# Latent attention: the query's norm applied as the scale of the softmax exponential, its sums of squares taken with the squares stationary

## The chip, the cores and the metric

One core of one Trainium2 chip runs the whole program as one launch. The metric is device time in microseconds of that core. Five engines work side by side and meet at semaphores: TensorE (PE in the profile, its weight loads PEld), VectorE (DVE), ScalarE (ACT), GpSimd (POOL) and SyncE (SP), which issues the weight transfers.

## The reference

Three transformer blocks over 16 meta tokens and 256 sequence tokens of width 1024, in float32: a state space mixer with an MLP, a latent attention mixer with an MLP, and a block with neighbourhood attention, a convolution branch and an MLP. The change is in the latent attention only:

```python
q = (rms_norm(q_lat, q_a_g) @ w_q_b).reshape(bsz, L, MLA_HEADS, MLA_QK)     # 16 heads of 96
...
q = rms_norm(q, q_norm_g)          # over the 96 values of a head
k = rms_norm(k, k_norm_g)
...                                # rope on the last 32 of the 96
sc = jnp.einsum('bqhd,bkhd->bhqk', q[:, s:e], k[:, :e]).astype(jnp.float32) * scale
p = jax.nn.softmax(jnp.where(mask, sc, -jnp.inf), axis=-1)
```

The norm of the query is one factor per token and head. A row of scores belongs to one query token, so the factor can be applied to the query (before) or to the whole row of scores (after).

## The kernel before

All activations lie transposed, features on the 128 partitions and tokens along the free axis (T = 272 tokens with the meta tokens, T2 = 256 without). A weight page of 128 x 1024 is split into two reduced-precision parts, `w_hi` on ACT and `w_lo` on DVE, and a product is three matmuls (hi x hi, hi x lo, lo x hi). Weight pages pass through four slots.

The latent attention is a hand-written pipeline of 22 steps t (`MLA_STEPS`). Each engine runs its own list of pieces in program order, and semaphores tie the lists together:

- `unit(t)` on PE, t = 0 to 15, makes the raw projection of two heads: keys and values at even t, queries at odd t. `unit_raw` on ACT squares it (`k_sq`, `q_sq`) and copies the value part (`v_t`) or the scaled query part (`q_pre`, L1076). On DVE, `keys` makes the scaled keys `k_pre` (L1560) at even t; `rotate` and `rotate_sum` apply the rope to the query at odd t. PE's next query unit waits for `k_pre` (`kpre_done`), since they share a PSUM bank.
- `unit_norm(t-1)` on PE sums the squares of a head over its 96 rows. For the query (L644) a 97 x 128 matrix of ones is stationary and the squares of 256 tokens move through; row 97 carries the epsilon of the latent's norm. All 128 output rows are the same sum. For the keys (L647) it is done the same way, and three transposes of the values per head (L649 to L651) follow.
- `unit_inv(t-1)` on ACT makes the inverse root: a logarithm (`n_ln`, L1091 for the query, L1096 for the key) and an exponential (`n_inv`, L1108 and L1111), each over 96 rows and 512 or 544 columns. For the keys two copies of the values stand between them. `finish(t-1)` on DVE multiplies: `q_fin` (L1569) and `k_fin` (L1574).
- `scores(t-3)` on PE (L664, L665), `maxima(t-4)` on DVE (L1581: adds the mask to the scores, negates, and keeps the row minimum, `nmx`), `exps(t-4)` on ACT (L1119: two exponentials with the maximum as bias and constant scale -1), `weigh(t-5)` on DVE, `p_transposes(t-6)` on PE (L678 to L682), copies of these to SBUF by ACT (`p_t0_copy`, L1127) and DVE (`p_t_copy`, L1599), `values` on PE for two heads at a time, `o_high` on ACT and `o_low` on DVE.

Order inside a step, which the prediction follows. ACT: `o_high` (even t), `unit_raw`, `p_t0_copy` (odd t, here), `unit_inv`, `exps`, `hi` (the next page's `w_hi`, L839), `p_t0_copy` (even t, here). DVE: `o_low` (even t), `lo` (`w_lo`, L1240), `maxima`, `p_t_copy` (odd t), `keys` or `rotate` with `rotate_sum`, `weigh`, `finish`, `p_t_copy` (even t). PE at even t: `unit`, `unit_norm`, `scores`, `p_transposes`; at odd t: `unit`, `p_transposes`, `unit_norm`, `scores`, `values`.

Of the kernel before, what the change touches and what calls it, by code (L numbers as in the profile page):

```python
# [14 lines left out]
F32 = mybir.dt.float32  # L15
# [131 lines left out]
def build(nc, w, h0, vec, const, rpb, out, acs_dram):  # L147
    ctx = ExitStack()
    with ctx:
# [73 lines left out]
        rot_a = sb("rot_a", [P, 2, T], F32, mla)  # L223
        rot_b = sb("rot_b", [P, 2, T], F32, mla)
        l_ln = rot_a
        q_pre = sb("q_pre", [QK, 4, T2], F32, mla)
        k_pre = sb("k_pre", [QK, 4, T], F32, mla)
        q_sq = sb("q_sq", [QK + 1, 4, T2], F32, mla)
        k_sq = sb("k_sq", [QK, 4, T], F32, mla)
# [103 lines left out]
        lh_done, ll_done, rope_done, krope = sem("lh_done"), sem("ll_done"), sem("rope_done"), sem("krope")  # L333
        raw_read, rot_done, rot_sum, nsum_done = sem("raw_read"), sem("rot_done"), sem("rot_sum"), sem("nsum_done")
        qsq_read, ksq_read, kpre_done = sem("qsq_read"), sem("ksq_read"), sem("kpre_done")
        erow_done, kpesq_done = sem("erow_done"), sem("kpesq_done")
        nln_done, ninv_done, fin_done = sem("nln_done"), sem("ninv_done"), sem("fin_done")
        s_done, sm_done, nm_done, ex_done = sem("s_done"), sem("sm_done"), sem("nm_done"), sem("ex_done")
        ri_done, p_done, pT_done, pt_done, pt0_done = (sem("ri_done"), sem("p_done"), sem("pT_done"),
# [56 lines left out]
        def _(pe):  # L396
# [230 lines left out]
            def unit_norm(un):  # L627

                is_q = un % 2
                ku, k = At(K_HEAD + 2 * un), At(K_HEAD + 2 * un + 1)  # L630
                free(k)
                if is_q:
                    pe.wait_ge(qsq_read, un // 2 + 1)
                    if un == 1:
                        pe.wait_ge(erow_done, 1)
                else:
                    pe.wait_ge(drained[ku.parity], ku.half + 1)
                    if un == 0:
                        pe.wait_ge(kpesq_done, 1)
                for j in range(2):  # L640
                    head = 2 * (un // 2 % 2) + j
                    bank = lin[:, 2 * k.parity + j, :]
                    if is_q:
                        ins = nc.tensor.matmul(bank[:, 0:T2], ones[0:QK + 1, :], q_sq[:, head, :],  # L644
                                               start=True, stop=True)
                    else:
                        nc.tensor.matmul(bank[:, 0:T], ones[0:QK, :], k_sq[:, head, :], start=True, stop=True)  # L647
                        idv = ident[HD:P, HD:P]
                        nc.tensor.transpose(bank[:, 272:336], v_t[HD:P, head, META:144], idv)  # L649
                        nc.tensor.transpose(bank[:, 336:400], v_t[HD:P, head, 144:T], idv)  # L650
                        ins = nc.tensor.transpose(bank[0:META, 400:464], v_t[HD:P, head, 0:META], idv)  # L651
                ins.then_inc(nsum_done, 1)

            def scores(n):
                s, j = n // 4, n % 4
                p = s % 2
                if n % 2 == 0:
                    pe.wait_ge(fin_done, n + 2)
                if n >= 2:
                    pe.wait_ge(sm_done, n - 1)  # L660
                elif n == 0:
                    pe.wait_ge(l_act, 1)
# [168 lines left out]
        def _(act):  # L831
# [237 lines left out]
            def unit_raw(un):  # L1069

                k = At(K_HEAD + 2 * un)
                act.wait_ge(w_used, 2 * C_HEAD + un + 1)
                hs = slice(2 * (un // 2 % 2), 2 * (un // 2 % 2) + 2)
                if un % 2:
                    a(q_sq[0:QK, hs, :], linp(k, slice(0, T2), slice(0, QK)), ACT.Square).then_inc(qsq_read, 1)
                    a(q_pre[0:HD, hs, :], linp(k, slice(0, T2), slice(0, HD)), ACT.Copy,  # L1076
                      scale=v(V_QG, rows=slice(0, HD))).then_inc(drained[k.parity], 1)
                else:
                    a(k_sq[0:HD, hs, :], linp(k, slice(0, T), slice(0, HD)), ACT.Square).then_inc(ksq_read, 1)
                    a(v_t[HD:P, hs, :], linp(k, slice(0, T), slice(HD, P)), ACT.Copy).then_inc(drained[k.parity], 1)  # L1080

            def unit_inv(un):

                s, is_q = un // 4, un % 2
                k = At(K_HEAD + 2 * un + 1)
                w_ = T2 if is_q else T
                if un >= 1:
                    act.wait_ge(ninv_done, un)
                act.wait_ge(nsum_done, un + 1)
                if is_q:  # L1090
                    a(n_ln[:, :, 0:w_], linp(k, slice(0, w_), slice(0, QK)), ACT.Ln, bias=eps_t[0:QK, 3:4],  # L1091
                      scale=1.0 / QK).then_inc(drained[k.parity], 1)
                else:
                    hp = un // 2 % 2
                    hs = slice(2 * hp, 2 * hp + 2)
                    a(n_ln[:, :, 0:w_], linp(k, slice(0, w_), slice(0, QK)), ACT.Ln, bias=eps_t[0:QK, 0:1],  # L1096
                      scale=1.0 / QK)
                    if s >= 2:
                        act.wait_ge(pv_done, 4 * (s - 2) + 2 * hp + 2)
                    a(v_tok[s % 2][:, hs, 1:3, :], linp(k, slice(272, 400)).rearrange("p h (t d) -> p h t d", d=HD),  # L1100
                      ACT.Copy)
                    a(v_tok[s % 2][0:META, hs, 0, :], linp(k, slice(400, 464), slice(0, META)), ACT.Copy)\
                        .then_inc(drained[k.parity], 1)
                act.wait_ge(drained[k.parity], k.half + 1)
                if un >= 1:
                    act.wait_ge(fin_done, un)
                if is_q:
                    a(n_inv[:, :, 0:w_], n_ln[:, :, 0:w_], ACT.Exp, scale=-0.5, bias=eps_t[0:QK, 1:2])\  # L1108
                        .then_inc(ninv_done, 1)
                else:  # L1110
                    a(n_inv[:, :, 0:w_], n_ln[:, :, 0:w_], ACT.Exp, scale=-0.5).then_inc(ninv_done, 1)  # L1111

            def exps(n):
                p = n % 2
                act.wait_ge(sm_done, n + 1)
                if n >= 3:
# [117 lines left out]
        def _(dve):  # L1234
# [310 lines left out]
            def rotate_sum(t):  # L1545

                un, h0_ = t // 2, 2 * (t // 2 % 2)
                dve.wait_ge(rot_done, 2 * un + 1)
                nc.vector.tensor_copy(rot_b[rr, :, 0:T2], rot_a[rs_, :, 0:T2]).then_inc(rot_done, 1)
                dve.wait_ge(rot_done, 2 * un + 2)  # L1550
                tt(q_pre[rr, h0_:h0_ + 2, :], rot_a[rr, :, 0:T2], rot_b[rr, :, 0:T2], ALU.add).then_inc(rot_sum, 1)

            def keys(t):

                un, h0_ = t // 2, 2 * (t // 2 % 2)
                k = At(K_HEAD + 2 * t)
                dve.wait_ge(ksq_read, un + 1)
                if t >= 4:
                    dve.wait_ge(fin_done, t - 3)
                ts(k_pre[0:HD, h0_:h0_ + 2, :], linp(k, slice(0, T), slice(0, HD)),  # L1560
                   v(V_KG, rows=slice(0, HD)), None, ALU.mult).then_inc(kpre_done, 1)

            def finish(un):
                s = un // 4
                dve.wait_ge(ninv_done, un + 1)
                hs = slice(2 * (un // 2 % 2), 2 * (un // 2 % 2) + 2)
                if un % 2:
                    dve.wait_ge(rot_sum, un // 2 + 1)
                    ins = tt(q_fin[s % 2][:, hs, :], q_pre[:, hs, :], n_inv[:, :, 0:T2], ALU.mult)  # L1569
                else:  # L1570
                    dve.wait_ge(kpre_done, un // 2 + 1)
                    if un == 0:
                        dve.wait_ge(krope, 3)
                    ins = tt(k_fin[s % 2][:, hs, :], k_pre[:, hs, :], n_inv[:, :, :], ALU.mult)  # L1574
                ins.then_inc(fin_done, 1)

            def maxima(n):
                p, o = n % 2, (ps5, ps6)[n % 2]
                dve.wait_ge(s_done, n + 1)
                for i, sl in enumerate((slice(0, 144), slice(144, 416))):  # L1580
                    ins = nc.vector.tensor_tensor_reduce(  # L1581
                        out=s_m[p][:, sl], in0=o[:, sl], in1=cst[:, N_MLA + sl.start:N_MLA + sl.stop], scale=-1.0,
                        scalar=3e38, op0=ALU.add, op1=ALU.min, accum_out=nmx[p][:, i:i + 1])
                ins.then_inc(sm_done, 1)

            def weigh(n):
                p = n % 2
# [17 lines left out]
            for t in range(MLA_STEPS + 1):  # L1605
# [394 lines left out]
```

## Time and profile before

| | us |
|---|---|
| median of 3 runs (lowest, highest) | 1151.34 (1149.97, 1151.72) |
| the profiled execution's own time | 1150.44 |
| its span, first to last instruction | 1148.8 |
| PE busy in the span | 1111.8 (97%) |
| PEld, DVE, ACT, POOL busy | 1068.5, 766.3, 672.6, 152.2 |
| mean granted clock of TensorE | 0.996 of 2.4 GHz |

The span is 1.6 us shorter than the profiled execution's time, and that execution is 0.9 us below the median. The latent attention's pipeline of steps lies at 477 to 590 us of the span. There PE was busy for 99.81 of 113.00 us, ACT for 81.63 and DVE for 78.99. Times in the rows are microseconds from the start of the span.

### The profile page before, as it was taken

The page shows a single profiled execution, that of the slowest core. Times are in us where ns is not written, and L with a number is a line of the kernel's source. Part 1 is how long each engine was busy: PE and PEld are TensorE (multiplying, and loading weights), DVE is VectorE, ACT ScalarE, POOL GpSimd, SP SyncE. Part 2 cuts the span into 40 slices and gives each one's busy share as a digit, 9 for nine tenths or more (in the row PEclk, how much of TensorE's full clock was granted, in tenths as well). Part 3 has the DMA queues.
Part 4 walks back from the last instruction along what each step waited for, and adds up shares of the span by engine and source line. Part 5 has one row for each costly group of instructions (what it writes and reads, how often), then busy time and mean ns, then how long its engine had stood idle before and what let it go on. Part 6 is the DMA issues. An engine that isn't in the chain of part 4 may idle for free.

```text
span 1148.8 us, 23776 instructions
## 1 busy us (share of the span) xinstructions
PE 1111.8 (97%) x8898; PEld 1068.5 (93%) x8898; DVE 766.3 (67%) x1122; ACT 672.6 (59%) x1071; POOL 152.2 (13%) x118
## 2 busy tenths in 40 slices
PE   6999999999999999899889999999999999999998
PEld 5989999999999999877689999999998999999998
DVE  4689999767665555678766665555687577666443
ACT  4789999655454434688655554445545656555332
POOL 0344443417000000100010000000001302000000
PEclk9999999999999999999999999999999999999999
DMA  5554454484555555333235555565544556555552
GB/s 201 172 181 164 150 185 147 139 247 165 183 170 177 165 182 175 123 110 108 74 108 186 183 185 188 175 197 172 174 138 128 189 175 188 188 184 186 191 183 91
DMA packets 53225, 190.32 MB, mean 166 GB/s; under 512 B 5920, under 2 KB 7072, under 8 KB 53168
## 3 DMA queue, kind: packets, MB, share of 16 engines
q1 hardware_dynamic: 51408, 182.95, 48.9%
q0 software_dynamic: 1760, 6.59, 1.8%
q8 instruction: 38, 0.62, 0.2%
q14 instruction: 19, 0.16, 0.0%
HBM read 188.44 MB, written 1.08 MB: 165 GB/s over the span
## 4 chain that ended last, share of the span: by engine, by line
PE 89%; DVE 6%; ACT 3%; issue 1%; DMA 0%; SPq 0%; ACTq 0%; DVEq 0%
PE lin L414 27%; PE lin L416 27%; PE lin L415 27%; DVE w_lo L1240 2%; ACT w_hi L839 1%; PE ps L507 1%; PE lin L647 1%; PE ps L447 1%; DVE x_lo L1250 0%; PE ps L665 0%; DVE cv L1320 0%; ACT pr L1167 0%; PE ps L695 0%; PE ps L693 0%; PE ps L510 0%
## 5 line engine op out<-in xcount | busy, mean ns | idle before, releaser
L1240 DVE TENSOR_TENSOR w_lo<-w_raw,w_hi 128x1024 fp32r<-128x1024 f32 (+2 forms) x319 | 387.2, 1215 | 281.4 <-ACT w_hi L839 281.2
L839 ACT ACTIVATE w_hi<-w_raw 128x1024 fp32r<-128x1024 f32 (+1 forms) x343 | 355.0, 1039 | 236.1 <-PE lin L416 234.1
L414 PE MATMUL lin<-x_hi,w_hi 128*128 128x256 f32 (+1 forms) x1528 | 442.7, 290 | 10.8 <-DVE cv L1320 4.1
L416 PE MATMUL lin<-x_hi,w_lo 128*128 128x256 f32 (+1 forms) x1528 | 436.6, 286 | 0.0
L415 PE MATMUL lin<-x_lo,w_hi 128*128 128x256 f32 (+1 forms) x1528 | 435.8, 285 | 0.0
L414 PEld LDWEIGHTS lin<-x_hi,w_hi 128*128 128x128 f32 x1528 | 289.5, 189 | 14.9 <-DVE cv L1320 4.6
L415 PEld LDWEIGHTS lin<-x_lo,w_hi 128*128 128x128 f32 x1528 | 289.0, 189 | 1.4 <-issue 1.0
L416 PEld LDWEIGHTS lin<-x_hi,w_lo 128*128 128x128 f32 x1528 | 289.8, 190 | 0.0
L416 PE MATMUL lin<-hid_hi,w_lo 128*128 128x256 f32 (+1 forms) x768 | 218.2, 284 | 0.0
L415 PE MATMUL lin<-hid_lo,w_hi 128*128 128x256 f32 (+1 forms) x768 | 217.9, 284 | 0.0
L414 PE MATMUL lin<-hid_hi,w_hi 128*128 128x256 f32 (+1 forms) x768 | 217.4, 283 | 0.0
L416 PEld LDWEIGHTS lin<-hid_hi,w_lo 128*128 128x128 f32 x768 | 145.2, 189 | 0.0
L414 PEld LDWEIGHTS lin<-hid_hi,w_hi 128*128 128x128 f32 x768 | 145.0, 189 | 0.0
L415 PEld LDWEIGHTS lin<-hid_lo,w_hi 128*128 128x128 f32 x768 | 144.4, 188 | 0.0
L1773 POOL TENSOR_TENSOR h_sq<-h_sq 128x256 f32<-128x256 f32 (+1 forms) x35 | 31.1, 890 | 554.1 <-ACT h_sq L852 552.7
L1007 ACT ACTIVATE relu<-lin 128x512 f32<-128x512 f32 (+1 forms) x48 | 29.1, 605 | 82.7 <-PE lin L416 82.7
L1784 POOL TENSOR_TENSOR w_lo<-w_raw,w_hi 128x1024 fp32r<-128x1024 f32 x24 | 59.0, 2459 | 86.1 <-ACT w_hi L839 86.0
L848 ACT ACTIVATE x_hi<-h,vecs 128x256 fp32r<-128x256 f32 (+2 forms) x40 | 20.3, 508 | 42.7 <-DVE h L1480 37.7
L1463 DVE TENSOR_TENSOR hid_lo<-relu_sq,hid_hi 128x512 f32 (+1 forms) x48 | 34.4, 717 | 11.2 <-DVE relu_sq L1459 11.2
L1320 DVE SCALAR_TENSOR_TENSOR cv<-lin,vecs,cv 128x271 f32<-128x271 f32 (+2 forms) x96 | 40.1, 477 | 0.0
L414 PE MATMUL lin<-g_hi,w_hi 128*128 128x272 f32 x128 | 37.8, 295 | 1.9 <-DVE g_lo L1364 1.0
L416 PE MATMUL lin<-g_hi,w_lo 128*128 128x272 f32 x128 | 37.0, 289 | 0.0
(265 smaller groups left out, 1469.5 us busy)
## 6 DMA issues: line engine op xcount, KB each, us to landing
w_raw<-w SPq DMA_DIRECT2D x343, 512.0 KB, 3.4
acs_bc<-acs_dram POOLq DMA_DIRECT2D x8, 544.0 KB, 4.9
bias_mask<-rpb POOLq DMA_DIRECT2D x4, 512.0 KB, 9.7
h<-h SPq DMA_DIRECT2D x4, 272.0 KB, 4.1
out<-h SPq DMA_DIRECT2D x8, 128.0 KB, 3.2
cst<-const SPq DMA_DIRECT2D x1, 784.0 KB, 8.9
vecs<-vec SPq DMA_DIRECT2D x1, 131.5 KB, 2.2
acs_dram<-y POOLq DMA_DIRECT2D x1, 34.0 KB, 2.1
```

The source lines that it names most:

```text
L414: mm3(o, wh, xh, start=first and i == 0, stop=False)
L415: mm3(o, wh, xl, start=False, stop=False)
L416: ins = mm3(o, wl, xh, start=False, stop=last and i == kts - 1)
L447: ins = nc.tensor.matmul(ps7[:, 0:T], ones0, h_sq[:, kt, :], start=kt == 0, stop=kt == KD - 1)
L839: a(w_hi[pg.slot][:, 0:n], w_raw[pg.slot][:, 0:n], ACT.Copy).then_inc(w_hi_done, pages)
L848: a(x_hi[:, kt.value, 0:width(norm)], h[:, kt.value, tokens(norm)], ACT.Copy, scale=gain(norm, kt.value)).then_inc(xh_done, 1)
L1007: a(relu[i][:, :, 0:n], linp(k, slice(0, n)), ACT.Relu).then_inc(drained[k.parity], 1)
L1240: tt(w_lo[pg.slot][:, 0:n], w_raw[pg.slot][:, 0:n], w_hi[pg.slot][:, 0:n].bitcast(F32), ALU.subtract)\
L1320: ins = stt(cv[:, q, back:T], lin[:, 2 * k.parity + i, 0:T - back], v(s.times(20, V_CONV + 5 * q + 3 - back).value), cv[:, q, back:T], ALU ...
L1463: tt(hid_lo[:, bass.ds(at.value, 2), 0:n], relu_sq[i][:, :, 0:n], hid_hi[:, bass.ds(at.value, 2), 0:n].bitcast(F32), ALU.subtract).then_in ...
L1773: tt(h_sq[:, 0, 0:n], h_sq[:, 0, 0:n], h_sq[:, kt, 0:n], ALU.add).then_inc(hsum_done, 1)
L1784: tt(w_lo[pg.slot][:, 0:n], w_raw[pg.slot][:, 0:n], w_hi[pg.slot][:, 0:n].bitcast(F32), ALU.subtract)\
```

## The change

The query is no longer normalized before the scores. `unit_raw` and `rotate_sum` write the scaled and rotated query straight into `q_fin`, and the multiplication L1569 is gone. The sums of squares are taken with the squares of 128 tokens stationary and one column of ones moving, so that they come out with tokens on the partitions: four matmuls of one column for two heads in place of two of 256 columns. The logarithm and exponential of `unit_inv` work on 128 x 4 values in place of 96 x 512. The scores are raw; `maxima` keeps the row maximum in `mx`, and a small added instruction multiplies it by minus the norm's factor `q_inv`, giving the bias; `exps` takes `q_inv` as its scale, a column of 128 values in place of the constant. The semaphores follow: `fin_done` counts keys only, and `scores` waits for the raw query's two parts.

```diff
+        q_ln = sb("q_ln", [P, 2, 2], F32, mla)
+        q_inv = sb("q_inv", [P, 8, 2], F32, mla)
+        mx = [sb(f"mx{i}", [P, 2], F32, mla) for i in range(2)]
...
                     if is_q:
-                        ins = nc.tensor.matmul(bank[:, 0:T2], ones[0:QK + 1, :], q_sq[:, head, :],
-                                               start=True, stop=True)
+                        for qt in range(2):
+                            at = 2 * j + qt
+                            ins = nc.tensor.matmul(lin[:, 2 * k.parity, at:at + 1],
+                                                   q_sq[:, head, qt * P:(qt + 1) * P], ones[0:QK + 1, 0:1],
+                                                   start=True, stop=True)
...
                 if n % 2 == 0:
-                    pe.wait_ge(fin_done, n + 2)
+                    kq = At(K_HEAD + 2 * (n + 1))
+                    pe.wait_ge(fin_done, n // 2 + 1)
+                    pe.wait_ge(rot_sum, n // 2 + 1)
+                    pe.wait_ge(drained[kq.parity], kq.half + 1)
...
-                    a(q_pre[0:HD, hs, :], linp(k, slice(0, T2), slice(0, HD)), ACT.Copy,
+                    if s >= 2:
+                        act.wait_ge(s_done, 4 * (s - 2) + hs.stop)
+                    a(q_fin[s % 2][0:HD, hs, :], linp(k, slice(0, T2), slice(0, HD)), ACT.Copy,
                       scale=v(V_QG, rows=slice(0, HD))).then_inc(drained[k.parity], 1)
...
                 if is_q:
-                    a(n_ln[:, :, 0:w_], linp(k, slice(0, w_), slice(0, QK)), ACT.Ln, bias=eps_t[0:QK, 3:4],
-                      scale=1.0 / QK).then_inc(drained[k.parity], 1)
+                    if un >= 2:
+                        act.wait_ge(qinv_done, un // 2)
+                    a(q_ln[:, :, :].rearrange("p h t -> p (h t)"), lin[:, 2 * k.parity, 0:4], ACT.Ln,
+                      bias=eps_t[:, 3:4], scale=1.0 / QK).then_inc(drained[k.parity], 1)
...
                 if is_q:
-                    a(n_inv[:, :, 0:w_], n_ln[:, :, 0:w_], ACT.Exp, scale=-0.5, bias=eps_t[0:QK, 1:2])\
-                        .then_inc(ninv_done, 1)
+                    at = 2 * (un // 2 % 4)
+                    a(q_inv[:, at:at + 2, :], q_ln[:, :, :], ACT.Exp, scale=-0.5, bias=eps_t[:, 1:2])\
+                        .then_inc(qinv_done, 1)
...
-                    ins = a(pr[n % 3][:, sl], s_m[p][:, sl], ACT.Exp, scale=-1.0, bias=nmx[p][:, i:i + 1],
+                    ins = a(pr[n % 3][:, sl], s_m[p][:, sl], ACT.Exp, scale=q_inv[:, n % 8, i:i + 1],
+                            bias=nmx[p][:, i:i + 1],
                             accum_out=rsum[p][:, i:i + 1])
...
-                tt(q_pre[rr, h0_:h0_ + 2, :], rot_a[rr, :, 0:T2], rot_b[rr, :, 0:T2], ALU.add).then_inc(rot_sum, 1)
+                s = t // 4
+                if s >= 2:
+                    dve.wait_ge(s_done, 4 * (s - 2) + h0_ + 2)
+                tt(q_fin[s % 2][rr, h0_:h0_ + 2, :], rot_a[rr, :, 0:T2], rot_b[rr, :, 0:T2], ALU.add)\
+                    .then_inc(rot_sum, 1)
...
-                if un % 2:
-                    dve.wait_ge(rot_sum, un // 2 + 1)
-                    ins = tt(q_fin[s % 2][:, hs, :], q_pre[:, hs, :], n_inv[:, :, 0:T2], ALU.mult)
...
-                        out=s_m[p][:, sl], in0=o[:, sl], in1=cst[:, N_MLA + sl.start:N_MLA + sl.stop], scale=-1.0,
-                        scalar=3e38, op0=ALU.add, op1=ALU.min, accum_out=nmx[p][:, i:i + 1])
-                ins.then_inc(sm_done, 1)
+                        out=s_m[p][:, sl], in0=o[:, sl], in1=cst[:, N_MLA + sl.start:N_MLA + sl.stop], scale=1.0,
+                        scalar=-3e38, op0=ALU.add, op1=ALU.max, accum_out=mx[p][:, i:i + 1])
+                ins.then_inc(mx_done, 1)
+                dve.wait_ge(qinv_done, n // 2 + 1)
+                dve.wait_ge(mx_done, n + 1)
+                stt(nmx[p][:, :], mx[p][:, :], -1.0, q_inv[:, n % 8, :], ALU.mult, ALU.mult).then_inc(sm_done, 1)
...
-                if 1 <= t <= 16:
+                if 1 <= t <= 16 and t % 2:
                     finish(t - 1)
```

## Rows read from the trace of the kernel before

**Rows 1.** Waits of 476 to 592 us: total us, times, longest us.

```profile
PE ps L678 <- ACT p_t L1127: 4.4, 4, 3.3
PE lin L414 <- DVE k_pre L1560: 1.8, 1, 1.8
```

**Rows 2.** Stretches: length, busy us (instructions) of PE, PEld, DVE, ACT, POOL; PEclk, DMA.

```profile
530.90:542.16 11.26, 10.87 (x74) 8.23 (x75) 9.37 (x26) 9.33 (x24) 0.00 (x0) 1.00 0.28 95
560.00:570.00 10.00, 6.15 (x35) 4.97 (x33) 6.77 (x20) 5.23 (x15) 0.00 (x0) 0.83 0.33 106
```

**Rows 3.** PE in order of time: start us, us, line and operation, count.

```profile
508.06 0.28 PE L416 MATMUL lin<-l_hi,w_lo 128*128 128x256 f32 x1
508.40 0.27 PE L678 MATMUL ps<-cst,pr 128*16 128x128 f32 x1
...
530.15 0.28 PE L415 MATMUL lin<-l_lo,w_hi 128*128 128x256 f32 x1
530.26 0.28 PE L416 MATMUL lin<-l_hi,w_lo 128*128 128x256 f32 x1
530.91 0.27 PE L678 MATMUL ps<-cst,h_sq 128*16 128x128 f32 x1 [0.37 <-ACT p_t L1127]
...
537.20 1.03 PE L644 MATMUL lin<-q_sq,cst 97*128 97x256 f32 x4
538.06 0.41 PE L664 MATMUL ps<-k_fin,q_fin 96*128 96x144 f32 x2
538.31 0.62 PE L665 MATMUL ps<-k_fin,q_fin 96*128 96x272 f32 x2
...
539.21 0.27 PE L682 MATMUL ps<-cst,pr 128*128 128x128 f32 x1
539.41 0.36 PE L414 MATMUL lin<-l_hi,w_hi 128*128 128x256 f32 x1
```

**Rows 4.** ACT in order of time, one pair of steps.

```profile
533.47 0.71 ACT L1096 ACTIVATE n_ln<-lin,eps_t 96x544 f32<-96x544 f32 x1 [1.40 <-PE lin L651]
534.35 0.25 ACT L1102 ACTIVATE v_tok<-lin 16x128 f32<-16x128 f32 x1
538.68 0.68 ACT L1091 ACTIVATE n_ln<-lin,eps_t 96x512 f32<-96x512 f32 x1
540.02 0.40 ACT L1119 ACTIVATE h_sq<-s_m,nmx 128x144 f32<-128x144 f32 x1
541.66 0.35 ACT L1127 ACTIVATE p_t<-ps 16x256 f32<-16x256 f32 x1
```

**Rows 5.** DVE in order of time: the maximum's last piece and what follows it.

```profile
538.54 0.09 DVE L1581 DVE_READ_ACCUMULATOR2_ANT nmx<- 128x1 f32 x1
538.54 0.77 DVE L1560 TENSOR_SCALAR k_pre<-lin,vecs 64x544 f32<-64x544 f32 x1
```

**Rows 6.** DVE in the later neighbourhood attention, where a maximum is negated.

```profile
831.50 0.08 DVE L1645 DVE_READ_ACCUMULATOR2_ANT mx<- 128x1 f32 x1
831.62 0.17 DVE L1650 TENSOR_SCALAR nmx<-mx 128x2 f32<-128x2 f32 x1
831.70 1.00 DVE L1713 SCALAR_TENSOR_TENSOR cv<-zc,vecs,cv 128x256 f32<-128x256 f32 x2
```

**Rows 7.** ACT by form, whole span: count | busy us, mean ns | idle before.

```profile
L909 ACT ACTIVATE cv<-lin,vecs 128x272 f32<-128x272 f32 x32 | 16.4, 563 | 0.0
L963 ACT ACTIVATE g_ln<-ps,eps_t 128x272 f32<-128x272 f32 x8 | 3.9, 482 | 5.2 <-PE ps L494 5.2
```

**Rows 8.** DVE and PE at the last gated query unit.

```profile
550.74 0.77 DVE L1560 TENSOR_SCALAR k_pre<-lin,vecs 64x544 f32<-64x544 f32 x1
551.62 0.36 PE L414 MATMUL lin<-l_hi,w_hi 128*128 128x256 f32 x1 [0.89 <-issue]
```

**Rows 9.** The tail: ACT, then PE, in order of time.

```profile
562.54 0.41 ACT L1119 ACTIVATE pr<-s_m,nmx 128x144 f32<-128x144 f32 x1 [0.88 <-DVE nmx L1581]
564.91 0.27 PE L678 MATMUL ps<-cst,h_sq 128*16 128x128 f32 x1 [3.27 <-ACT p_t L1127]
```

More of the change, by code:

```diff
@@ L225, in build @@
         l_ln = rot_a
-        q_pre = sb("q_pre", [QK, 4, T2], F32, mla)
+        q_ln = sb("q_ln", [P, 2, 2], F32, mla)
+        q_inv = sb("q_inv", [P, 8, 2], F32, mla)
+        mx = [sb(f"mx{i}", [P, 2], F32, mla) for i in range(2)]
         k_pre = sb("k_pre", [QK, 4, T], F32, mla)
@@ L335, in build @@
         qsq_read, ksq_read, kpre_done = sem("qsq_read"), sem("ksq_read"), sem("kpre_done")
-        erow_done, kpesq_done = sem("erow_done"), sem("kpesq_done")
+        erow_done, kpesq_done, qinv_done, mx_done = sem("erow_done"), sem("kpesq_done"), sem("qinv_done"), sem("mx_done")
         nln_done, ninv_done, fin_done = sem("nln_done"), sem("ninv_done"), sem("fin_done")
@@ L1074, in unit_raw @@
                 if un % 2:
+                    s = un // 4
                     a(q_sq[0:QK, hs, :], linp(k, slice(0, T2), slice(0, QK)), ACT.Square).then_inc(qsq_read, 1)
-                    a(q_pre[0:HD, hs, :], linp(k, slice(0, T2), slice(0, HD)), ACT.Copy,
+                    if s >= 2:
+                        act.wait_ge(s_done, 4 * (s - 2) + hs.stop)
+                    a(q_fin[s % 2][0:HD, hs, :], linp(k, slice(0, T2), slice(0, HD)), ACT.Copy,
                       scale=v(V_QG, rows=slice(0, HD))).then_inc(drained[k.parity], 1)
@@ L1085, in unit_inv @@
                 k = At(K_HEAD + 2 * un + 1)
-                w_ = T2 if is_q else T
-                if un >= 1:
-                    act.wait_ge(ninv_done, un)
                 act.wait_ge(nsum_done, un + 1)
                 if is_q:
-                    a(n_ln[:, :, 0:w_], linp(k, slice(0, w_), slice(0, QK)), ACT.Ln, bias=eps_t[0:QK, 3:4],
-                      scale=1.0 / QK).then_inc(drained[k.parity], 1)
-                else:
+                    if un >= 2:
+                        act.wait_ge(qinv_done, un // 2)
+                    a(q_ln[:, :, :].rearrange("p h t -> p (h t)"), lin[:, 2 * k.parity, 0:4], ACT.Ln,
+                      bias=eps_t[:, 3:4], scale=1.0 / QK).then_inc(drained[k.parity], 1)
+                else:
+                    if un >= 2:
+                        act.wait_ge(ninv_done, un // 2)
                     hp = un // 2 % 2
                     hs = slice(2 * hp, 2 * hp + 2)
-                    a(n_ln[:, :, 0:w_], linp(k, slice(0, w_), slice(0, QK)), ACT.Ln, bias=eps_t[0:QK, 0:1],
+                    a(n_ln[:, :, :], linp(k, slice(0, T), slice(0, QK)), ACT.Ln, bias=eps_t[0:QK, 0:1],
                       scale=1.0 / QK)
@@ L1104, in unit_inv @@
                 act.wait_ge(drained[k.parity], k.half + 1)
-                if un >= 1:
-                    act.wait_ge(fin_done, un)
                 if is_q:
-                    a(n_inv[:, :, 0:w_], n_ln[:, :, 0:w_], ACT.Exp, scale=-0.5, bias=eps_t[0:QK, 1:2])\
-                        .then_inc(ninv_done, 1)
-                else:
-                    a(n_inv[:, :, 0:w_], n_ln[:, :, 0:w_], ACT.Exp, scale=-0.5).then_inc(ninv_done, 1)
+                    at = 2 * (un // 2 % 4)
+                    a(q_inv[:, at:at + 2, :], q_ln[:, :, :], ACT.Exp, scale=-0.5, bias=eps_t[:, 1:2])\
+                        .then_inc(qinv_done, 1)
+                else:
+                    if un >= 2:
+                        act.wait_ge(fin_done, un // 2)
+                    a(n_inv[:, :, :], n_ln[:, :, :], ACT.Exp, scale=-0.5).then_inc(ninv_done, 1)
             def exps(n):
@@ L1558, in keys @@
                 if t >= 4:
-                    dve.wait_ge(fin_done, t - 3)
+                    dve.wait_ge(fin_done, t // 2 - 1)
                 ts(k_pre[0:HD, h0_:h0_ + 2, :], linp(k, slice(0, T), slice(0, HD)),
@@ L1564, in finish @@
                 s = un // 4
-                dve.wait_ge(ninv_done, un + 1)
+                dve.wait_ge(ninv_done, un // 2 + 1)
                 hs = slice(2 * (un // 2 % 2), 2 * (un // 2 % 2) + 2)
-                if un % 2:
-                    dve.wait_ge(rot_sum, un // 2 + 1)
-                    ins = tt(q_fin[s % 2][:, hs, :], q_pre[:, hs, :], n_inv[:, :, 0:T2], ALU.mult)
[L1570 to L1575, printed above, removed]
+                dve.wait_ge(kpre_done, un // 2 + 1)
+                if un == 0:
+                    dve.wait_ge(krope, 3)
+                tt(k_fin[s % 2][:, hs, :], k_pre[:, hs, :], n_inv[:, :, :], ALU.mult).then_inc(fin_done, 1)
             def maxima(n):
```

## The prediction

> **What bounds the kernel now.** I read the page's busy shares first: PE is busy for 97% of the span, so over the whole program only what moves PE counts. The change touches only the latent attention's steps, 113 us long. There I read the waits, and then laid one pair of steps (a key unit and a query unit) out engine by engine.
>
> One pair takes 11.26 us, and PE is busy for 10.87 of them, ACT for 9.33 and DVE for 9.37 [rows 2]. PE waits once per pair in plain sight, for ACT's small copy of the transposed probabilities before L678 [rows 1, 3]. The last matmul of the query unit starts at 530.26 and L678 at 530.91, which is 0.65 us; a matmul of this kind hands over after 0.11 to 0.12 us [rows 3], so 0.53 us are lost. The same gap stands ahead of 519.66 and 542.16, and a smaller one of 0.34 - 0.12 = 0.22 us ahead of 508.40 [rows 3].
>
> The second gate is nearly hidden. Each query unit waits for DVE's `k_pre`. In the pair shown `k_pre` starts at 538.54 and lasts 0.77 us, so it ends at 539.31, and the unit starts at 539.41 [rows 3, 5]. At the last query unit it ends at 551.51, and the unit starts at 551.62, 0.11 us later [rows 8]; there the profile calls the 0.89 us of idle time "issue", but the constant lag to `k_pre` tells what it is. The six query units 5, 7, ... 15 all start 0.10 or 0.11 us after the end of `k_pre`. In three of them (9, 11, 13) PE would itself have been ready only some 0.1 us earlier (L682 starts at 539.21 and holds PE for 0.11), in the others it idles longer. So whatever makes `k_pre` later moves PE one for one, and whatever makes it earlier gives almost nothing in those three.
>
> What stands before `k_pre`? PE's last value transpose L651 releases ACT, which had been idle for 1.40 us [rows 4]. ACT then makes the key's `n_ln`, two copies, `n_inv`, the two exponentials of `exps`, `w_hi` and `o_hi`; DVE follows with `o_lo`, `w_lo`, the maximum, and `k_pre`. None of the query's norm lies in this chain. It lies in the other one, from the end of PE's key unit through ACT's `k_sq`, `v_t`, query `n_ln`, `n_inv`, `exps`, `w_hi` and the copy L1127 to PE's L678.
>
> **The change part by part.** *The query's norm on ACT.* From the start of `n_ln` at 538.68 to the start of `exps` at 540.02 are 1.34 us [rows 4]. Two instructions of 4 columns take their place. The trace has none of that size with 128 partitions; the nearest is the copy of 16x128 at 0.25 us [rows 4]. I take 0.25 each, 0.5 for both with the wait between them, so 0.84 goes. The ends are nothing for both and 0.7 (0.08 more each for the bias column, worked out below), so between 0.64 and 1.34 goes. Of this `exps` gives 0.16 back (below). PE's gap of 0.53 needs no more than 0.53, and PE itself comes later by the terms that follow, so the gap closes at either end. What is late next at L678 is PE itself. The relief is 3 x 0.53 + 0.22 = **-1.8 us**. After the last query unit, in the tail, ACT's query norm lies in time in which ACT then waits for the maximum anyway (0.88 us idle [rows 9]), and gives nothing.
>
> *The multiplication L1569 on DVE* (0.69 us, eight times) stands behind `k_pre` and `weigh`; the copy behind it lies 0.3 us ahead of PE. It hides behind PE and gives nothing to the gates. Writing into `q_fin` straight away costs the same as into `q_pre`. Its new waits, for scores of two head groups earlier, and those of `scores` for the raw query of two steps earlier, were met long before: nothing.
>
> *The small instruction after the maximum.* In the later attention the same pattern exists: the read-out starts at 831.50, the negation at 831.62, the next instruction at 831.70 [rows 6]. Before, `k_pre` starts with the read-out (both 538.54 [rows 5]), so the price is 0.20 us in front of `k_pre`. Its ends are 0.08 (if the wait cost nothing) and 0.35 (the 0.12 of the wait, the whole 0.17 of the instruction and another wait of 0.05, since two semaphores are waited for). I take 0.20, the same pattern. Queued behind it on DVE are `k_pre`, for which PE waits, and everything up to `weigh`. It is paid at query units 5, 7, 9, 11, 13, 15, and once in the tail, where ACT waits for the maximum [rows 9] and PE for ACT (3.27 us [rows 9]): 7 x 0.20 = **+1.4 us**.
>
> *The scale of the exponential as a column.* An activation of 128x272 from PSUM with scale and bias columns takes 563 ns, one with the bias column alone 482 [rows 7]: 0.08 us per instruction, with an end of 0 (another function and output might explain the difference) and of 0.1. Two exponentials stand in the chain before `k_pre` of query units 7, 9, 11, 13, 15, and four in the tail's chain (one pair delays `w_hi`, `o_hi` and `w_lo`, the next, at 562.54 [rows 9], stands before L1127): 14 x 0.08 = **+1.1 us**. The Trainium skill states this price (ScalarE: Activation LUTs, section What ACT_TABLE_LOAD costs): each column operand adds about 93 ns over an immediate. It speaks against the change, and the trace's 81 ns bears it out; by the page's figure this term would be 1.3 us and my sum 0.2 us higher.
>
> *The sums on PE.* Before, four matmuls (each product of plain float32 takes two) from 537.20 to 538.06, 0.86 us [rows 3]. After, eight, each with its own load of 97x128. The nearest pitch with such a load is that of L664, 0.25 us for two at 144 columns [rows 3], so 8 x 0.125 = 1.0 us by this row. No row has one moving column: the low end is nothing at all, the high end 0.27 each (the whole duration of L678 [rows 3]), 2.2 us. I take 1.0, +0.14 for each query unit, as the same load decides it. It doesn't show: between the sums and the next query unit PE is going to wait for `k_pre`, 0.1 us already and 0.36 more by the two terms above, so 0.45 of cover. Cheaper matmuls would be hidden by the same wait. Were the cover gone, it would be 8 x 0.14 = 1.1 us.
>
> **Sum.** -1.8 + 1.4 + 1.1 = +0.7 us against the profiled execution's 1150.44, 1151.1 us. Since that execution lies 0.9 below the median of 1151.34, the forecast for the median is 1152.0. ACT would be less busy by about 5 us and DVE by about 3, and PE would not gain.
>
> **The rivals.** *A: the late chain has slack that I don't see*, and the relief stays whole, with the small instruction and the scale column hidden: 1151.34 - 1.8 = 1149.5. For it: ACT and DVE are busy for only 83% of a pair [rows 2]. Against it: the constant 0.1 us lag at six units.
>
> *B: the one-column matmuls are dear.* On PE, between the query's squares and the next `scores`: if load and multiplication of one column don't overlap as those of 144 columns do, each takes a pitch p of its own. The cover of 0.45 is used up from 8p = 0.86 + 0.45, p = 0.163 us. At the high end, p = 0.27, each of some seven units adds 2.16 - 1.31 = 0.85, and the time is 1152.0 + 5.9 = 1157.9. Against it: L664 has 0.125 with the same load. The Trainium skill (TensorE: Matmul & The Clock Gate, section LDWEIGHTS) prices a load of 128 columns at 107 ns whatever the rows, which would make eight of them 0.86 us, no change; no row here has one moving column.
>
> *C: the relief doesn't come*, because L678 waits for DVE's copy and the probabilities once ACT is out of the way, while all prices are paid: 1151.34 + 2.5 = 1153.8. It decides if that copy ends over 0.3 us later than now in relation to PE's query unit. Against it: 0.69 us of multiplication goes from in front of it.
>
> *D: the clock.* After PE's idle 3.3 us in the tail the granted clock is 0.83 on average at 560 to 570 [rows 2], as 3.4 us at the lower level (1.2 GHz) give it, and PE loses 10 x 0.17 = 1.7 us of work. If that stretch isn't there after the change: 1152.0 - 1.7 = 1150.3. If PE's longer waits bring a second one, 1153.7.
>
> **How the numbers follow.** Forecast 0.55, its own range 1151.2 to 1152.9 (the ends of the wait and of the scale column). A 0.18, B 0.08, C 0.08, D without the stretch 0.07, with a second 0.04. A measurement of this kernel tells 0.2%, 2.3 us, from no change, so faster is below 1149.0 and slower above 1153.6. Slower: half of B's, C's and the second stretch's 0.20, and a little of the forecast's upper end, 0.13. Faster: the lower end of A and A with D, 0.06. Same 0.81. The range 1149.4 to 1153.9 takes in A, most of C and D, and leaves out B.
>
> **What would show it.** Right: the wait of L678 for ACT's L1127 shrinks from 4.4 us to the tail's alone, 3.3 to 3.7; query units start 0.10 us after `k_pre`, and that starts 0.2 us after the read-out; L1119 at 272 columns goes from 507 to about 590 ns; a pair of steps takes 11.1 us. Wrong: a pair of 10.7 us (A), a pitch over 0.16 us in L644's successors (B), L678 waiting for DVE (C). The prediction is wrong as a whole if the attention's steps change by more than 2 us either way.

## The result and the profile after

The changed kernel takes 1155.12 us (median of 6 executions, 1153.89 to 1156.76) against 1151.17 us for the kernel before, timed beside it: a ratio of 1.0033 with a 95% interval of [1.0023, 1.0043]. It is slower by 3.9 us, where 0.7 was forecast, and lies above the range's end of 1153.9. A second comparison (e1 below) gives 1.0026 [1.0015, 1.0038], 3.0 us.

The profiled execution took 1154.64 us (span 1153.0), 4.2 us above the one of before; 0.7 of them had come about before the attention's first query unit (478.56 against 477.81), the rest lies in the attention. ACT's 669.3 busy us are 3.3 fewer and DVE's 764.3 are 2.0 fewer, somewhat less than the 5 and 3 forecast. PE's 1116.3 are 4.5 more, which no part of the sum had. First the waits of 476 to 592 us:

```profile
PE ps L686 <- ACT p_t L1141: 3.7, 1, 3.7
PE lin L416 <- issue: 4.7, 6, 1.4
PE lin L416 <- DVE k_pre L1578: 1.8, 1, 1.8
```

Of four waits for ACT's small copy [rows 1] only the tail's is left. The six waits put down to "issue" are the query units, which now visibly wait for the key scaling. One pair of steps on PE (start us, us, what, idle before):

```profile
533.29 0.28 PE L418 MATMUL lin<-l_hi,w_lo 128*128 128x256 f32 x1
533.41 0.27 PE L686 MATMUL ps<-cst,h_sq 128*16 128x128 f32 x1
...
539.70 0.95 PE L648 MATMUL lin<-cst,q_sq 97*128 97x1 f32 x8
540.51 0.49 PE L672 MATMUL ps<-k_fin,q_fin 96*128 96x144 f32 x2
...
541.73 0.27 PE L690 MATMUL ps<-cst,pr 128*128 128x128 f32 x1
542.34 0.36 PE L416 MATMUL lin<-l_hi,w_hi 128*128 128x256 f32 x1 [0.33 <-issue]
```

L686 follows the query unit's last matmul after 0.12 us, where it took 0.65 [rows 3]: the relief is whole. Eight one-column products take 0.81 us (539.70 to 540.51), 0.10 each, a little less than the 0.86 of before. The query unit starts 0.61 us after L690, where it took 0.20 [rows 3]. DVE at the same place:

```profile
541.17 0.08 DVE L1594 DVE_READ_ACCUMULATOR2_ANT mx<- 128x1 f32 x1
541.35 0.16 DVE L1600 SCALAR_TENSOR_TENSOR nmx<-mx,q_inv 128x2 f32<-128x2 f32 x1
541.46 0.78 DVE L1578 TENSOR_SCALAR k_pre<-lin,vecs 64x544 f32<-64x544 f32 x1
```

The key scaling starts 0.29 us after the last read-out, not with it [rows 5], and ends at 542.24, 0.10 before PE's unit. The two prices on ACT (by form, 476 to 592 us: count | busy, mean ns | idle before):

```profile
L1132 ACT ACTIVATE pr<-s_m,nmx,q_inv 128x272 f32<-128x272 f32 x11 | 6.6, 599 | 0.0
L1119 ACT ACTIVATE q_inv<-q_ln,eps_t 128x4 f32<-128x4 f32 x8 | 2.4, 297 | 0.3
L1101 ACT ACTIVATE q_ln<-lin,eps_t 128x4 f32<-128x4 f32 x8 | 2.1, 262 | 0.2
```

The exponential of 272 columns went from 507 ns to 599, and the query's pair of activations to 0.26 and 0.30 us.

So far everything is as argued, but for the small instruction's 0.29 us in place of 0.20. What the sum didn't have stands in the clock (stretches of 5 and 12 us: length, busy us of PE, PEld, DVE, ACT, POOL with instructions, PEclk, DMA share, GB/s). Before:

```profile
497.00:502.00 5.00, 5.00 (x35) 3.98 (x35) 3.89 (x10) 3.93 (x10) 0.00 (x0) 1.00 0.45 156
562.00:574.00 12.00, 9.09 (x60) 7.79 (x60) 6.78 (x26) 5.01 (x16) 0.00 (x0) 0.86 0.28 88
```

and after:

```profile
497.00:502.00 5.00, 4.75 (x24) 4.25 (x25) 2.20 (x8) 2.36 (x6) 0.00 (x0) 0.66 0.54 192
562.00:574.00 12.00, 7.60 (x41) 6.22 (x40) 6.61 (x21) 5.68 (x16) 0.00 (x0) 0.72 0.26 88
```

At 497 to 502 the granted clock is 0.66 on average, 3.4 us at 1.2 GHz where before had none, and in the tail it is 0.72 in place of 0.86, 6.8 us at the lower level in place of 3.4. PE makes 24 matmuls in the first stretch in place of 35.

To compare kernels free of what happens in the program's start I use the **stage**: from the start of query unit 1 (477.81 before) to the first matmul after PE's last wait of the attention (590.33 before). Before it is 112.5 us, after 594.55 - 478.56 = 116.0. In the table each median has the kernel before's, timed beside it, in brackets; the ratio is taken over the executions and isn't the quotient of the two medians (in e6 it is 0.9998, the quotient 0.9993).

| kernel | median us (before beside it) | ratio [95%] | stage us | low-clock stretches in the stage: start (length) |
|---|---|---|---|---|
| before | 1151.17 | | 112.5 | 565 (3.4) |
| after | 1155.12 (1151.17) | 1.0033 [1.0023, 1.0043] | 116.0 | 498 (3.4), 566 (6.8) |
| e1 after again | 1154.59 (1151.6) | 1.0026 [1.0015, 1.0038] | 115.9 | 496 (3.4), 564 (6.8) |
| e2 128 moving columns | 1153.71 (1151.6) | 1.0020 [1.0011, 1.0028] | 113.8 | 567 (3.4) |
| e3 prices only | 1154.00 (1151.6) | 1.0022 [1.0013, 1.0031] | 115.7 | 567 (6.8) |
| e4 before, one column | 1154.32 (1151.6) | 1.0024 [1.0012, 1.0035] | 115.2 | 497 (3.4), 565 (6.8) |
| e5 e2, keys first | 1152.51 (1151.07) | 1.0010 [1.0002, 1.0019] | 113.6 | 567 (3.4) |
| e6 before, keys first | 1150.25 (1151.07) | 0.9998 [0.9989, 1.0006] | 112.0 | 565 (3.4) |
| e7 e6, step 16 | 1150.80 (1151.07) | 1.0001 [0.9992, 1.0010] | 111.6 | 565 (3.4) |
| e8 e5, step 16 | 1151.08 (1151.07) | 1.0000 [0.9991, 1.0009] | 114.9 | 479 (3.4), 564 (6.8) |
| e9 wide at unit 3 alone | 1154.57 (1151.42) | 1.0032 [1.0020, 1.0045] | 116.9 | 488 (3.4), 509 (3.4), 567 (6.8) |
| e10 one column at unit 3 alone | 1154.55 (1151.42) | 1.0035 [1.0021, 1.0048] | 116.0 | 498 (3.4), 566 (6.8) |
| e11 32 columns | 1154.69 (1151.42) | 1.0030 [1.0018, 1.0042] | 115.9 | 498 (3.4), 566 (6.8) |
| e12 e2, negated on GpSimd | 1152.17 (1151.42) | 1.0005 [0.9996, 1.0014] | 113.3 | 563 (6.8) |

The stretches come from one profiled execution each. A second look at them is the mean granted clock over all timed executions: 0.9937 to 0.9942 for the kernel before (76 executions beside e1 to e12; three far slower ones, 1215 to 1345 us at a mean clock of 0.76 to 0.85, are left out), 0.990 to 0.991 for each of the kernels with narrow sums (after, e1, e4, e9, e10, e11), 0.992 to 0.994 for e2, e3, e5 to e8 and e12. The executions also split the difference without any trace: at a mean clock of 0.993 the four of the changed kernel (after and e1) average 1153.7 us and the 31 of the kernel before 1152.0. So about 1.7 us of the 3.0 to 3.9 are there at equal clock, and the rest goes with the clock. This is an estimate, since the clock is on record to 0.001 and that much goes with 0.5 us (the kernel before averages 1150.5 at 0.996).

### The profile page after: what moved, and what is told of

Same layout as the page of the kernel before. It is cut to its first block, busy times and chain, and to the rows that moved or that the text cites. A ratio compares the mean times of both kernels' runs of the same rounds, so it can differ in the third digit from the quotient of the medians.

```text
span 1153.0 us, 23859 instructions
## 1 busy us (share of the span) xinstructions
PE 1116.3 (97%) x8930; PEld 1074.6 (93%) x8930; DVE 764.3 (66%) x1130; ACT 669.3 (58%) x1071; POOL 152.3 (13%) x118
## 4 chain that ended last, share of the span: by engine, by line
PE 91%; DVE 5%; ACT 2%; issue 1%; DMA 0%; SPq 0%; ACTq 0%; DVEq 0%
PE lin L416 28%; PE lin L418 27%; PE lin L417 27%; DVE w_lo L1254 2%; PE ps L509 1%; ACT w_hi L847 1%; PE lin L652 1%; PE ps L449 1%; PE ps L673 0%; DVE cv L1334 0%; ACT pr L1181 0%; PE ps L672 0%; PE ps L703 0%; PE ps L701 0%; PE lin L648 0%
## 5 line engine op out<-in xcount | busy, mean ns | idle before, releaser
L1254 DVE TENSOR_TENSOR w_lo<-w_raw,w_hi 128x1024 fp32r<-128x1024 f32 (+2 forms) x319 | 387.1, 1215 | 283.1 <-ACT w_hi L847 282.8
L1477 DVE TENSOR_TENSOR hid_lo<-relu_sq,hid_hi 128x512 f32 (+1 forms) x48 | 34.4, 716 | 11.2 <-DVE relu_sq L1473 11.2
```

Source lines behind the costliest of these rows:

```text
L1254: tt(w_lo[pg.slot][:, 0:n], w_raw[pg.slot][:, 0:n], w_hi[pg.slot][:, 0:n].bitcast(F32), ALU.subtract)\
L1477: tt(hid_lo[:, bass.ds(at.value, 2), 0:n], relu_sq[i][:, :, 0:n], hid_hi[:, bass.ds(at.value, 2), 0:n].bitcast(F32), ALU.subtract).then_in ...
```

## The experiments

My theory once the two traces lay side by side: the gates behave as predicted, and the rest is the clock, which falls where PE's sums have one moving column and stand next to a wait. The rivals: the added prices lengthen PE's waits and that lowers the clock, or the difference lies in the start of the program, where the two traces differ too.

**e1.** No edit.

> The changed kernel once more, for a second trace and for the clock of more executions. Its first trace has 6.8 us at the lower clock in the attention's tail and 3.4 us at 498 to 501 us, where the kernel before had 3.4 and none. Theory 'clock' (the change makes PE fall to 1.2 GHz more often in the attention's steps): the ratio is again 1.003 to 1.004, and a low stretch lies somewhere among the head units again. Rival 'start' (the low stretches of the program's first 60 us, which differ between the two traces, make the difference, by luck of one build or one chip): the ratio falls to 1.001, and the mean clock of the executions is that of the kernel before (0.995).

The ratio fell a little, but stays clear of 1.001, and the stretch is there again at 496. In this trace the start has 3.4 us twice, as in the kernel before, and the stage is the same as in the first (115.9). So the start is not the cause of what the stage shows.

**e2.** 128 columns move through.

```diff
-                            at = 2 * j + qt
+                            at = (2 * j + qt) * P
-                            ins = nc.tensor.matmul(lin[:, 2 * k.parity, at:at + 1],
-                                                   q_sq[:, head, qt * P:(qt + 1) * P], ones[0:QK + 1, 0:1],
+                            ins = nc.tensor.matmul(lin[:, 2 * k.parity, at:at + P],
+                                                   q_sq[:, head, qt * P:(qt + 1) * P], ones[0:QK + 1, :],
...
-                    a(q_ln[...], lin[:, 2 * k.parity, 0:4], ACT.Ln, ...
+                    a(q_ln[...], lin[:, 2 * k.parity, 0:4 * P:P], ACT.Ln, ...
```

> The changed kernel with 128 identical moving columns of ones in place of one in the query's sums (ACT reads every 128th column of the result). PE then works for the full 0.86 us per query unit, not 0.8 us with one column per load. Theory 'one column' (products of one column count as idle for the clock): the extra low stretches vanish and the time is 1.0 to 1.5 us above the kernel before (1152 to 1152.7). Rival 'waits' (the added price before the key scaling and in the tail lengthens PE's waits, and that brings the low clock): as the changed kernel, 1155.

The stretch is gone:

```profile
497.00:502.00 5.00, 3.99 (x27) 2.95 (x25) 3.44 (x11) 3.56 (x9) 0.00 (x0) 1.00 0.46 126
562.00:574.00 12.00, 7.60 (x47) 5.84 (x46) 6.61 (x21) 5.35 (x16) 0.00 (x0) 0.86 0.28 88
```

Query unit 7 starts 10.1 us after unit 5; in after it is 11.65, so the stretch costs 1.5 us. The whole stage is 113.8, 1.2 us above before: that is the change without its added low-clock stretches. By medians the kernel is still 2.1 us above before, not 1.5 at most, and only 0.9 below e1, with intervals that overlap: the times alone don't show what the wide sums give back, the stage does. Its trace has 3.4 us of low clock at 595, just behind the stage, which the kernel before doesn't have, and its executions have a lower mean clock (0.992).

**e3.** The two prices on the kernel before.

```diff
-                        ..., scale=-1.0, scalar=3e38, op0=ALU.add, op1=ALU.min, accum_out=nmx[p][:, i:i + 1])
-                ins.then_inc(sm_done, 1)
+                        ..., scale=1.0, scalar=-3e38, op0=ALU.add, op1=ALU.max, accum_out=mx[p][:, i:i + 1])
+                ins.then_inc(mx_done, 1)
+                dve.wait_ge(ninv_done, 2 * (n // 2) + 2)
+                dve.wait_ge(mx_done, n + 1)
+                stt(nmx[p][:, :], mx[p][:, :], -1.0, cst[:, N_ONES:N_ONES + 2], ALU.mult, ALU.mult)...
...
-                    ins = a(..., ACT.Exp, scale=-1.0, bias=nmx[p][:, i:i + 1], ...
+                    ins = a(..., ACT.Exp, scale=cst[:, N_ONES:N_ONES + 1], bias=nmx[p][:, i:i + 1], ...
```

> The kernel before with the two prices alone: the maximum kept positive and negated by a small instruction, and the exponential's scale as a column (of ones). The norm stays on the query as before. By the sum of the prediction, with the measured 0.29 us for the small instruction in place of 0.20: 7 x 0.29 + 14 x 0.09 = +3.3 us, less nothing, since the gap at the small copy stays: 1154.5. Theory 'waits' for the clock: 1.7 to 3.4 us more, 1156 to 1158, with a low stretch among the head units. Theory 'one column': 1154.5 without one.

1154.0 for 1154.5, and no stretch at 497, although PE idles longer ahead of query units 5 and 7 (1.09 and 1.51 us) than in the changed kernel (1.01 and 1.44):

```profile
497.00:502.00 5.00, 4.39 (x30) 3.49 (x31) 3.49 (x9) 3.85 (x9) 0.00 (x0) 1.00 0.39 111
```

A pair of steps takes 11.45 us, 0.2 more than before, not 0.47: as the query unit comes later, PE's wait for ACT shrinks by itself. Its matmul after the query unit:

```profile
532.65 0.28 PE L417 MATMUL lin<-l_hi,w_lo 128*128 128x256 f32 x1
533.02 0.27 PE L679 MATMUL ps<-cst,h_sq 128*16 128x128 f32 x1
```

0.37 us here, 0.65 before [rows 3], 0.12 after. This tells what the shorter norm on ACT is worth once the prices are paid: 0.25 of the 0.53 us; the rest went by the lateness alone. In the tail this trace has 6.8 us at the low clock in place of 3.4, without narrow sums.

**e4.** The one-column matmuls of the change in the kernel before (the hunk of `unit_norm` alone). The kernel leaves the query's norm out in effect, since the logarithm still reads the place where the wide sums stood.

> The kernel before with the query's sums made as in the changed kernel (squares stationary, one moving column, four numbers per pair of heads); the logarithm then reads mostly old values of the bank, so this kernel leaves the query's norm out in effect, and all durations and waits but PE's stay. Theory 'one column': slower by 1.7 to 3.5 us, 1153 to 1154.7, with a low stretch among the head units or a longer one in the tail. Rival 'waits': no change, 1151.2, since PE's sums are hidden behind its wait for the scaled keys.

```profile
493.87 0.95 PE L646 MATMUL lin<-cst,q_sq 97*128 97x1 f32 x8
494.68 0.49 PE L667 MATMUL ps<-k_fin,q_fin 96*128 96x144 f32 x2
495.01 0.62 PE L668 MATMUL ps<-k_fin,q_fin 96*128 96x272 f32 x2
496.39 0.36 PE L414 MATMUL lin<-l_hi,w_hi 128*128 128x256 f32 x1 [0.76 <-issue]
```

```profile
497.00:502.00 5.00, 5.00 (x26) 3.89 (x25) 3.29 (x9) 2.59 (x7) 0.00 (x0) 0.66 0.43 160
```

The one edit makes the kernel 2.7 us slower and brings the stretch, with PE's idle time ahead of the query unit as before (0.76 us, 0.78 before). The sums themselves take 0.81 us, less than before. Nothing but the sums was edited, so the 2.7 us (1.4 to 4.0 by the interval) are theirs. Of the stage's 2.6 us, 1.5 go with the stretch at 497 (query unit 7 starts 11.24 us after unit 5, 9.70 before) and 1.0 with the longer one in the tail.

**e5.** DVE, even steps: `keys(t)` moved ahead of `maxima(t - 4)`, on e2.

> The changed kernel with 128 moving columns (as e2) and, on DVE at even steps, the key scaling ahead of the maximum. Theory 'gate' (the price of the small instruction and of the scale column is paid at the key scaling, for which each later query unit waits): 0.9 us leave that chain, so query units 5, 7 and 15 start 0.9 us earlier and 9, 11, 13 by the 0.4 us that PE idles there; the maximum comes later and ACT's small copy with it, which takes back 0.2 us three times. In all -3.2 us against e2, 1150.5. Rival 'elsewhere' (the prices are paid at L678 or on ACT): -1 us or less, 1152.7 or more.

The chain to the key scaling did shorten: query unit 5 starts 8.3 us after unit 3 (9.1 in e2), unit 7 another 9.4 (10.1). But the stage is only 0.2 us shorter. PE's wait for ACT came back; from matmul to matmul it is 0.70 us, where I had reckoned with some 0.3:

```profile
542.37 0.28 PE L418 MATMUL lin<-l_hi,w_lo 128*128 128x256 f32 x1
543.07 0.27 PE L686 MATMUL ps<-cst,pr 128*16 128x128 f32 x1 [0.43 <-ACT p_t L1141]
```

and the way from query unit 15 to the tail's L686 takes 15.0 us, 1.1 more. Both ends of the expectation missed: the gate is real, but right behind it ACT holds the pair at 11.2 us.

**e6.** The same move in the kernel before.

> The kernel before with the key scaling ahead of the maximum at even steps. Theory 'gate': query units 5, 7 and 15 start 0.6 us earlier, 9, 11 and 13 are held by L678's wait for ACT anyway: -1.8 us, 1149.8. If instead the lag of 0.10 us to the key scaling is a coincidence: no change. The difference between e5 and this kernel is what the change is worth once the gate is away: by the theory -1.6 to 0 us for the norm on the scale (the relief at L678), plus 0.09 us per exponential in the tail.

The stage is 0.6 us shorter and the ratio holds no difference. Units 5 and 7 come earlier, by 0.6 us each as expected, so the lag was no coincidence, but the pairs stay at 11.26 us, and unit 9 (0.4 us) and the tail's L678 (0.7) give part of it back. Of the 1.8 us expected, 0.6 came.

**e7, e8.** In step 16 the maximum ahead of `lo`, the small copy ahead of `hi`, on e6 and e5.

> e6 and, in step 16 alone, the maximum ahead of the weight part on DVE and the small copy ahead of the weight part on ACT. PE's idle stretch before the tail's L678 shrinks from 3.3 to about 1.3 us. If idle time of PE is what brings the low clock in the tail, the 3.4 us at 1.2 GHz after it vanish: -2.0 - 1.7 = -3.7 us against e6, 1146.1. If the low stretch stays, -2.0, 1147.8.

> e5 with the same reordering of step 16. The tail's idle stretch goes from 3.9 to about 1.5 us: -2.4 for the wait and -1.7 to -2.4 for the low clock, 1146.1 against e5's 1150.5. With the gate away and the clock kept, the change should be level with e7 or up to 1 us faster; if it is slower than e7 by over 1 us, something beside the gates and the clock is paid.

Neither came: e7 takes 1150.8 us where at most 1147.8 was expected, e8 1151.1 for 1146.1. In e8, for one, the matmul that waited 3.72 us for ACT in the changed kernel now waits for DVE's copy:

```profile
565.18 0.37 PE L686 MATMUL ps<-cst,h_sq 128*16 128x128 f32 x1 [2.38 <-DVE p_t L1617]
```

The wait in e7 fell by 0.6 us only, the low stretch stayed at 3.4 us in e7 and at 6.8 in e8, and the medians are level with the kernel before. e8's trace also has a low stretch at 479, ahead of the first query sums: it begins 1.5 us behind a wait of 1.8 us that all kernels have. So narrow sums are not the only way to a low stretch. The tail's clock was not cured, and these two tell nothing sure on it.

**e9, e10.** The width chosen by unit: `wide = P if un == 3 else 1`, and `1 if un == 3 else P`.

> The changed kernel with 128 moving columns in the sums of query unit 3 alone, the last sums before PE waits for the start of query unit 5, and one column in the other seven. Theory 'one column next to a wait' (one-column products and the wait after them together let PE look idle): no low stretch at 496 to 501 us; time as e2, 2.1 to 2.4 us above the kernel before. Rival 'one column anywhere': the stretch stays, 3.0 us above.

> The reverse: one moving column in the sums of query unit 3 alone, 128 in the other seven. Theory 'one column next to a wait': the low stretch of 3.4 us at 496 to 501 is there, query unit 7 starts 11.6 us after query unit 5 instead of 10.1, and the time is that of the changed kernel, 3.0 us above the kernel before. Rival 'one column anywhere' (the sum of all eight units' missing work counts): no stretch, 2.2 above.

e9, five stretches from 487 us:

```profile
487.00:492.00 5.00, 3.49 (x17) 3.52 (x18) 2.33 (x3) 2.18 (x5) 0.00 (x0) 0.66 0.45 130
...
497.00:502.00 5.00, 3.98 (x29) 3.23 (x29) 3.48 (x13) 3.66 (x10) 0.00 (x0) 1.00 0.35 108
...
507.00:512.00 5.00, 3.57 (x20) 3.24 (x18) 4.66 (x16) 3.57 (x10) 0.00 (x0) 0.69 0.35 105
```

e10:

```profile
487.00:492.00 5.00, 4.01 (x28) 3.15 (x28) 2.75 (x5) 2.86 (x6) 0.00 (x0) 1.00 0.56 174
...
497.00:502.00 5.00, 4.86 (x24) 4.38 (x25) 2.17 (x8) 2.33 (x5) 0.00 (x0) 0.66 0.54 190
...
507.00:512.00 5.00, 3.57 (x29) 3.07 (x27) 4.59 (x17) 3.93 (x11) 0.00 (x0) 1.00 0.32 105
```

The stretch follows the narrow sums. With unit 3 wide it left 497 and came up behind the waits after units 1 and 5, whose sums are narrow in e9. With unit 3 alone narrow it is at 498 and nowhere else among the units. e9's time of 1.0032 was not foreseen (I expected e2's), since I hadn't thought of the other two waits.

Yet narrow sums next to a wait don't bring the stretch each time. PE idles for 0.7 us or more ahead of query units 3, 5, 7 and 15. Over all traces there are 20 such places behind sums with 1 or 32 columns, and 7 have a low stretch that begins within 0.7 us of the query unit's start; in the changed kernel only the one at unit 5 has it, though the waits at 3, 7 and 15 are longer. There are 24 such places behind sums with 128 or 256 columns, and none has it. What decides between the places with narrow sums stays open.

**e11.** `wide = 32`.

> The changed kernel with 32 moving columns in all query sums. PE's pitch stays that of the load, 0.10 us a product, as with one column (64 passes in 6.5 us against 6.9 us at 128 columns). If it is the columns that pass which keep the clock, a quarter of the work may be too little and the stretch at 496 to 501 stays (11.6 us from query unit 5 to 7); if any real stream of columns does, it goes (10.1 us).

```profile
497.00:502.00 5.00, 4.32 (x21) 3.99 (x21) 2.29 (x7) 2.26 (x6) 0.00 (x0) 0.66 0.56 166
```

In this trace 32 columns do no more for the clock than one.

**e12.** The negation and multiplication on GpSimd, as two small instructions in place of one, on e2. GpSimd had nothing to do in these steps. `maxima` gets two waits more, so that it doesn't overwrite what is still read.

```diff
-                dve.wait_ge(qinv_done, n // 2 + 1)
-                dve.wait_ge(mx_done, n + 1)
-                stt(nmx[p][:, :], mx[p][:, :], -1.0, q_inv[:, n % 8, :], ALU.mult, ALU.mult).then_inc(sm_done, 1)
...
+                for i in range(2):
+                    ins = ts(nmx[p][:, i:i + 1], mx[p][:, i:i + 1], q_inv[:, n % 8, i:i + 1], -1.0,
+                             ALU.mult, ALU.mult)
+                ins.then_inc(sm_done, 1)
```

> [...] The 0.29 us of the small instruction leave the chain to the key scaling: DVE's key scaling starts with the read-out again, and query units 5 and 7 each start 0.29 us sooner after the one before (8.84 and 9.84 us in place of 9.13 and 10.13). But the bias reaches ACT later by what GpSimd needs beyond DVE. If that is under 0.3 us the exponentials at even steps hardly wait, and the time is 1 to 1.7 us below e2; if it is 0.5 us or more, PE's wait moves to L678's successor and the gain is under 0.5 us.

DVE's key scaling starts with the read-out again:

```profile
538.99 0.08 DVE L1597 DVE_READ_ACCUMULATOR2_ANT mx<- 128x1 f32 x1
538.99 0.77 DVE L1578 TENSOR_SCALAR k_pre<-lin,vecs 64x544 f32<-64x544 f32 x1
```

Units 5 and 7 start 8.85 and 9.83 us after the ones before, as expected to 0.01 us, and the median is 0.8 us above before in place of e2's 2.1. The tail gives some back: the way from unit 15 to its L686 is 14.7 us, 13.85 in e2. The pairs take 10.87 us, 0.4 less than before: with the small instruction off DVE the relief does show. In the tail its trace has 6.8 us at the low clock. This form is level with the kernel before [0.9996, 1.0014], as is e8 [0.9991, 1.0009]; no form of the change beat it.

## Why the prediction was wrong

*The relief* was sized 0.53 us a pair and came whole; the wait is gone in all four places. e3 shows that half of it would have come by lateness alone, a point that the sum didn't need.

*The small instruction* was put at 0.20 us and costs 0.29, within its ends. The neighbourhood attention's pattern has one wait, here there are two; that this is the reason was not tested. 7 x 0.09 = 0.6 us of the miss.

*The scale column* was put at 0.08 per instruction and costs 0.09 (599 - 507 ns).

*The sums on PE* are the step that failed. Their duration lay inside its bounds (0.81 us against the 1.0 I took, and 0.86 before) and it was hidden, as I wrote. From "it doesn't show" I concluded that the step costs nothing. It costs the clock: e4 has the sums alone and loses 2.7 us by medians, 2.6 in the stage.

*The gates together* were to give +0.7. Without the clock's part they gave 1.2 (the stage of e2), close to +0.7 with the 0.6 of the small instruction. By medians e2 is 2.1 us above before; the 0.9 us that its stage doesn't hold stay open.

*Rival D*, the clock, named a second low stretch and its price of 1.7 us, but put it down to longer waits and gave it 0.04. e3 has longer waits and no stretch at 497; e4 has the same waits and the stretch. Of the others, A wanted a pair of 10.7 us and it is 11.15, B a pitch over 0.16 us and it is 0.10, C a wait of L686 for DVE and there is none in the pairs. My sign for being wrong as a whole, steps that change by more than 2 us, did come: 3.5.

Of the stage's 3.5 us, then, 1.2 are gates, 1.5 the stretch at 497, and 0.7 the longer one in the tail (10.60 us from its L686 at 568.28 to the next that waits, 578.88; 9.91 in e2, 9.97 before). This sum, from one trace, agrees with the medians' 3.0 and 3.9. That narrow sums at unit 3 bring the stretch at 497 is settled: it is there in all five traces with narrow sums at unit 3 (after, e1, e4, e10, e11) and in none of the nine others. Five of these nine (before, e2, e3, e9, e12) have PE idle there for 0.7 to 1.1 us as well; e5 to e8 hardly have the wait. Why the tail's stretch is 6.8 us in some kernels and 3.4 in others stays open. All six traces with narrow sums have 6.8, e10 too, whose sums near the tail are wide; e4 has 6.8 with the idle time of before, e3 and e12 have 6.8 with wide sums, e2 and e5 have 3.4 with idle time as long as e3's; one execution each can't tell it.

## What to carry to other kernels

A matmul's time in the profile is not all that it does: products with few moving columns look busy (0.95 us here) but next to a wait they can let PE's clock fall, and the price is paid by the matmuls that follow. When an edit makes PE's work lighter in a stage where PE also waits, price the clock as a term of its own, and look at PEclk in 5 us stretches before and after. Where two chains meet in a wait at nearly the same time, as here the key scaling and ACT's copy, shortening one gives only the distance to the other (e5, e6).

## What the runs showed of the hardware

Matmuls with 97x128 float32 weights follow each other by 0.10 us with 1 moving column (after) and with 32 (e11), so up to there the columns don't set the pace; with 128 columns (e2) it is 0.11. Behind sums with 1 or 32 columns and 0.7 to 1.6 us of idle time the granted clock fell to 1.2 GHz for 3.4 us at 7 of 20 places, behind sums with 128 or 256 columns at none of 24. The 3.4 us cost 1.5 us where PE was busy throughout (e4). A column operand for an activation's scale, besides one for its bias, costs 0.09 us (507 to 599 ns; 600 in e3, where the column is ones). A dependent small DVE instruction that waits on two semaphores adds 0.29 us in front of what follows; on GpSimd each of its two parts takes 0.28 us (e12), off DVE's path.
